# A diffusion step on one core: the value projections in 512 moving columns

## The reference

```
p = h @ w_in + b_in
(mq, mk, mv, mo, mi, mf, cb, cc, ch, nq, nk, nv, gt) = split(p)
y_ml = head_rms(mlstm_bidir(mq, mk, mv, ...)) * sigmoid(mo)
y_na = attention(nq, nk, nv, context cache, bias)
y_cv = cb * short_conv(cc * ch)
```

## Time and profile before

| | us |
|---|---|
| median of 3 runs | 3045.52 |
| lowest, highest | 3039.61, 3046.49 |
| the profiled execution | 3044.11 |
| its span | 3042.3 |
| TensorE busy | 2907.7 (96%) |
| VectorE, ACT, GpSimd busy | 1775.2 (58%), 1372.1 (45%), 544.8 (18%) |

### The profile page before, as it was taken

One profiled execution on the slowest core, in us unless ns is written; L12 is line 12 of the kernel. 1 busy time (PEld: TensorE's weight loads), 2 busy tenths in 40 slices (PEclk: granted clock), 3 DMA queues, 4 the chain that ended last, 5 costly groups with the idle time before them and its releaser, 6 DMA issues.

```text
span 3042.3 us, 41344 instructions
## 1 busy us (share of the span) xinstructions
PE 2907.7 (96%) x17186; PEld 2364.0 (78%) x17186; DVE 1775.2 (58%) x2039; ACT 1372.1 (45%) x1759; POOL 544.8 (18%) x215
## 2 busy tenths in 40 slices
PE   5999999999989999999989999999999899999998
PEld 4979888888976666767669798999998667676765
DVE  3550335134347889897966513351242798889897
ACT  2153321111137777776750533201101776777775
POOL 2504313232320000000024143242332100000000
PEclk9999999999999999999999899999999999999999
DMA  9423545475518989897975234423343597989896
GB/s 265 82 42 70 102 127 153 153 195 152 187 30 300 347 283 345 276 347 265 345 227 91 38 66 98 85 42 58 72 80 118 180 346 277 345 287 343 284 340 231
DMA packets 333691, 583.84 MB, mean 192 GB/s; under 512 B 14208, under 2 KB 98176, under 8 KB 333376
## 3 DMA queue, kind: packets, MB, share of 16 engines
q1 hardware_dynamic: 291312, 500.21, 54.6%
q10 hardware_dynamic: 33888, 60.04, 6.0%
q0 software_dynamic: 8304, 20.95, 2.1%
HBM read 567.49 MB, written 9.45 MB: 190 GB/s over the span
## 4 chain that ended last, share of the span: by engine, by line
PE 83%; DMA 5%; DVE 4%; ACT 3%; issue 2%; POOL 1%; SPq 1%; DVEq 1%; ACTq 0%; POOLq 0%
PE ps L861 26%; PE ps L1369 10%; PE ps L1372 10%; PE ps L1377 9%; PE ps L825 6%; PE ps L905 3%; PE ps L1138 2%; PE ps L1286 2%; DMA ring<-w_down 2%; DMA arena<-ada_w 2%; DMA ring<-w_gate 1%; PE ps L1119 1%; PE ps L929 1%; PE ps L1036 1%; PE ps L887 1%
## 5 line engine op out<-in xcount | busy, mean ns | idle before, releaser
L2344 DVE TENSOR_TENSOR w_lo<-ring,w_hi 128x2048 fp32r<-128x2048 f32 x256 | 583.9, 2287 | 97.4 <-ACT w_hi L1496 97.0
L1496 ACT ACTIVATE w_hi<-ring 128x2048 fp32r<-128x2048 f32 x256 | 487.0, 1910 | 81.3 <-DMA ring<-w_up 24.6
L861 PE MATMUL ps<-h_hi,w_hi 128*128 128x320 f32 x1632 | 511.2, 313 | 6.2 <-POOL w_lo L700 3.4
L861 PE MATMUL ps<-h_lo,w_hi 128*128 128x320 f32 x1632 | 507.7, 311 | 0.0
L861 PE MATMUL ps<-h_hi,w_lo 128*128 128x320 f32 x1632 | 507.7, 311 | 0.0
L698 POOL CAST w_hi<-ring 128x2048 fp32r<-128x2048 f32 (+1 forms) x74 | 141.3, 1910 | 1463.5 <-PE ps L1377 644.9
L700 POOL TENSOR_TENSOR w_lo<-ring,w_hi 128x2048 fp32r<-128x2048 f32 (+1 forms) x74 | 345.2, 4665 | 41.9 <-issue 36.2
L861 PEld LDWEIGHTS ps<-h_hi,w_hi 128*128 128x128 f32 x1632 | 309.7, 190 | 12.6 <-issue 9.9
L2344 DVE TENSOR_TENSOR w_third<-ring,w_third 128x2048 fp32r<-128x2048 f32 x128 | 293.1, 2290 | 40.8 <-ACT w_third L1496 40.0
L1559 ACT ACTIVATE arena<-ps,par 128x640 f32<-128x640 f32 x80 | 63.4, 795 | 561.7 <-PE ps L861 548.2
L861 PEld LDWEIGHTS ps<-h_lo,w_hi 128*128 128x128 f32 x1632 | 309.8, 190 | 0.0
(11 more groups left out here) (334 smaller groups left out, 5481.8 us busy)
## 6 DMA issues: line engine op xcount, KB each, us to landing
ring<-w_gate SPq DMA_DIRECT2D x128, 1024.0 KB, 6.2
ring<-w_up SPq DMA_DIRECT2D x128, 1024.0 KB, 6.0
ring<-w_down SPq DMA_DIRECT2D x128, 1024.0 KB, 6.9
ring<-w_in SPq DMA_DIRECT2D x64, 1024.0 KB, 13.1
arena<-ada_w ACTq DMA_DIRECT2D x40, 1024.0 KB, 7.0
arena<-ada_w SPq DMA_DIRECT2D x8, 1024.0 KB, 15.9
arena<-biasT ACTq DMA_DIRECT2D x16, 512.0 KB, 5.7
ring<-w_o SPq DMA_DIRECT2D x8, 1024.0 KB, 11.8
```

What stands on the lines that cost most here:

```text
L861: last = pe.matmul(ps[:, bank(u) + half, 0:HALF], w[:, k, f0:f0 + P], a[:, k, at], start=(k == 0 and part == 0), stop=(k == KD - 1 and par ...
L1496: act.activation(w_his[g % NW], ring[:, ff_slot(l, g), :], ACT.Copy).then_inc(ff_hi_ready.sem, 1)
L2344: dve.tensor_tensor(w_los[g % NW], ring[:, s, :], w_his[g % NW].bitcast(F32), ALU.subtract).then_inc(slot_used[s], 1)
```

## The change

`project_tokens` is turned inside out. A chunk of V's weights is now four k tiles of all 512 columns (rows 0 to 511 of `w_in`, then rows 512 to 1023) and a matmul has 512 columns. All five tiles take the first chunk, then all five the second, so five banks are open at once: tile 4 takes the odd bank beside tile 0's (`token_bank`). The first chunk is done with at tile 0 of the second round and the second at tile 4, and `ends` says so. On GpSimd the split of the first convolution chunk moves from behind the band loads to ahead of the stores of the attention's V.

```diff
+        def token_bank(u0, t):
+            return bank(u0 + t) if t < 4 else bank(u0) + 1
...
         for j in range(2):
-            ends[R_MV + j], ends[R_NV + j] = U_MV + NTILE - 1, U_NV + NTILE - 1
+            ends[R_MV + j], ends[R_NV + j] = U_MV + 4 * j, U_NV + 4 * j
...
-                        load(l, q + j, rows_of(win_l, c + CC * j))
+                        if q in (R_MV, R_NV):
+                            load(l, q + j, rows_of(w_in[l, 512 * j:512 * (j + 1), :], c, 512))
+                        else:
+                            load(l, q + j, rows_of(win_l, c + CC * j))
...
                 split(l, R_NV)
+                split(l, R_CONV, 1)
...
                 band_load(0)
                 band_load(1)
-                split(l, R_CONV)
+                split(l, R_CONV + 1, 1)
...
-                two = {}
-                for t, j in [(t, 0) for t in range(4)] + [(t, 1) for t in range(4)] + [(4, 0), (4, 1)]:
-                    if j == 0:
-                        free_unit(l, u0 + t)
-                    if j not in two:
-                        two[j] = split_chunk(l, q + j)
-                    _, hi, lo = two[j]
-                    at = slice(t * P, (t + 1) * P)
-                    for k in range(KD):
-                        for part, (a, w) in enumerate(((h_hi, hi), (h_lo, hi), (h_hi, lo))):
-                            last = pe.matmul(ps[:, bank(u0 + t), j * CC:(j + 1) * CC], a[:, k, at], w[:, k, :],
-                                             start=(k == 0 and part == 0), stop=(k == KD - 1 and part == 2))
-                    if j == 1:
-                        last.then_inc(unit_full.sem, 1)
+                for kh in range(2):
+                    for t in range(NTILE):
+                        if kh == 0 and t < 4:
+                            free_unit(l, u0 + t)
+                        if t == 0:
+                            hi, lo = (w.rearrange("p k n -> p (k n)").rearrange("p (k n) -> p k n", n=512)
+                                      for w in split_chunk(l, q + kh)[1:])
+                        at = slice(t * P, (t + 1) * P)
+                        for k in range(4):
+                            kk = 4 * kh + k
+                            for part, (a, w) in enumerate(((h_hi, hi), (h_lo, hi), (h_hi, lo))):
+                                last = pe.matmul(ps[:, token_bank(u0, t), :], a[:, kk, at], w[:, k, :],
+                                                 start=(kk == 0 and part == 0), stop=(kk == KD - 1 and part == 2))
+                        if kh == 1:
+                            last.then_inc(unit_full.sem, 1)
```

More of the change, by code:

```diff
@@ L2056, in norm_heads, with add_row_bias @@
                         .then_inc(head_normed.sem, 1)
-            def add_row_bias(l, u, out, at):
-                dve.wait_ge(*filled(l, u))
-                return dve.tensor_tensor(out, ps[:, bank(u), :], par[:, Q_BV + at:Q_BV + at + WB], ALU.add)
+            def add_row_bias(l, u0, t, out, at):
+                dve.wait_ge(*filled(l, u0 + t))
+                return dve.tensor_tensor(out, ps[:, token_bank(u0, t), :], par[:, Q_BV + at:Q_BV + at + WB], ALU.add)
             def attention(l):
@@ L2445, in _ @@
                     dve.tensor_tensor(mvx[:, t, :, 0:P],
-                                      ps[:, bank(U_MV + t), :].rearrange("p (h v) -> p h v", h=HM),
+                                      ps[:, token_bank(U_MV, t), :].rearrange("p (h v) -> p h v", h=HM),
                                       par[:, Q_BV:Q_BV + WB].rearrange("p (h v) -> p h v", h=HM), ALU.add)\
@@ L2462, in _ @@
                     out = nvp if t == 0 else nvst[:, t % 2, :]
-                    add_row_bias(l, U_NV + t, out, WB).then_inc(dve_emptied.sem, 1)
+                    add_row_bias(l, U_NV, t, out, WB).then_inc(dve_emptied.sem, 1)
                     dve.drain()
```

## The result

| | before | after |
|---|---|---|
| median, us | 3039.61 (5 runs) | 3055.05 (5 runs) |
| lowest, highest | 3033.63, 3046.49 | 3054.84, 3062.17 |
| the profiled execution, its span | 3044.11, 3042.3 | 3054.84, 3053.0 |

The change makes the kernel slower: the ratio is 1.0045, with a 95% interval of 1.0026 to 1.0064. The prediction's sum was 3054.9, its range 3041 to 3064.

What follows compares the result with a forecast made beforehand. TensorE, busy 96% of the span, was taken as the bound. From the profiled 3044.11 us: mLSTM blocks -2.4, attention starts +8.7 and +9.3, stall -2.4 twice, together +10.8, giving 3054.9; range 3041 to 3064.

Steps and rivals of the forecast that it cites:

- The matmuls: Value projections: 512-column matmuls at 230 ns, 1.2 us less a block; 2.4 us gained over the two mLSTM blocks.
- The Trainium skill's 131 ns: Sustained 512-column matmul pace: a block would take some 15.7 us, the sum 3031; the prediction judged the trace against it.
- The mLSTM's split: Split of the O gate's first chunk runs earlier, beside TensorE's V work; costed at nothing.
- The split ahead of the stores: Before attention: tile 1's store issued 4.4 us late and landing 4.9 us slower; starts lose 8.7 and 9.3 us.
- the landing: Tile 1's store, issue to landing: 6.4 and 7.55 us plus 4.9 for the ring load; upper end 9.7 more.
- Rivals 1 and 2: Ring load beside stores: first, stores untouched, 3045, 33%; second, bias loads held back and stores land faster, 3037, 7%.
- rival 1: Before attention: the ring load might be served first and does not touch the stores; sum 3045, chance 33%.
- The Trainium skill's turns between queues: DMA engines take equal turns among three queues: landing 9.6 us, 3.2 more instead of 4.9; sum 3051.5.
- The stall: First convolution piece no longer waits for w_lo; VectorE stays held, so 2.4 us gained in each layer.
- The distance that I took as fixed: From attention's start to the second chunk's subtraction: unchanged in the new order, so VectorE stays held and the gain is 2.4.
- The sum: mLSTM blocks -2.4, attention starts +8.7 and +9.3, stall -2.4 twice: +10.8 us, 3054.9; chance 54%.

Runs made afterwards that it cites:

- e1: The changed kernel with the first convolution split put back behind the band loads, 512 columns kept; ratio to the kernel before 1.0004.
- e2: The changed kernel with the ring load held until the stores of tiles 1 and 2 have landed; ratio to the kernel before 1.0054.
- e4: The changed kernel with ring load and bias loads both held until the stores of tiles 1 and 2 have landed; ratio to the kernel before 1.0019.
- e9: The kernel before (256 columns) with bias loads held and the cast's semaphore replacing the drain in the two convolution splits; ratio to the kernel before 0.9961.
- e3: The changed kernel with only the bias loads held until the stores of tiles 1 and 2 have landed; ratio to the kernel before 1.0038.
- e8: The changed kernel with split back behind band loads, bias loads held, cast's semaphore replacing the drain in both convolution splits; ratio to before 0.9937, median 3022.94 us.
- e11: e8 run once more, on the same chip as e9; ratio to the kernel before 0.9919, median 3019.53 us.

## Why the prediction held, and where it did not

The cause is the one predicted, and the sum came out within a us of the median; its terms did not all hold. The mechanism is shown by e1 (the split's move is the whole loss) and by e2 and e4 (the store's landing sets the start of attention).

**1. The matmuls.** 226.8 ns, the upper of the two gains considered (the extrapolated 227, not the measured 230 of the experts): 1.6 us a block instead of 1.2. It counts in the mLSTM and not in the attention's block, as said; e9 shows that it counts there once the store is out of the way. The Trainium skill's 131 ns ("TensorE: Matmul & The Clock Gate", "Back-to-back issue gap") is not met in this kernel.

**2. The mLSTM's split.** Nothing in layer 0: from 115.35 to the next block at 308.88 the kernel after took 193.5 us, before from 115.12 to 310.23 195.1, and the 1.6 between them is the block. In layer 1 the difference is 2.4 us; the 0.8 beyond the block goes with TensorE's granted clock, 0.75 over 13 us of the mLSTM's stage before (1687 to 1700) and 0.84 after (1688 to 1701).

**3. The split ahead of the stores.** VectorE's L2064 was held 3.92 us and ended 0.7 us behind the subtraction (predicted 0.55); the store went out at +26.1 from the block's start (predicted +25.7). The term that was mis-sized is the landing: 16.1 us in both layers, against 11.3 and 12.5. I had added the ring load's own DMA time, 4.9; the row of a bias load that had met ring loads said 9.7, and it was right (16.1 - 6.4 = 9.7 in layer 0, 16.1 - 7.55 = 8.6 in layer 1). My reason for not taking it, that there two loads had been freed ahead and here one, was wrong: e3 and e4 show that one is enough, and in that row, too, only one went ahead. The two ring loads of the kernel before were issued at 359.33 and 365.90, the bias load at 359.4. The first of them landed after 15.9 us, where the one with nothing beside it took 8.1; the price of such a meeting stood in the trace. SP's timeline, and landings of ring loads issued from 340 to 362 and from 305 to 330:

```profile
359.33 6.93 SPq L643 DMA_DIRECT2D ring<-w_in  x2
```

```profile
ring<-w_in SPq DMA_DIRECT2D x1, 1024.0 KB, 15.9
...
ring<-w_in SPq DMA_DIRECT2D x1, 1024.0 KB, 8.1
```

So what failed is the step that priced the meeting at the 4.9 us of DMA time that a ring load needs alone. The same 1040 packets now took 48.6% of 27 us (325 to 352), 13.1 us of all 16 engines, and the stores came behind them:

```profile
q1 hardware_dynamic: 1040, 1.05, 48.6%
```

Attention started at +44.0 where the prediction's sum has +38.7 and +39.8, so the starts cost 14.0 and 13.5 us, not 8.7 and 9.3. Rivals 1 and 2 fall with it: the ring load was served first, as rival 1 has it, but at a pace that made the stores wait. The Trainium skill's turns between queues ("DMA: Bandwidth & Descriptors", "Queues, rings and completion order"), read as equal time, gave 3.2 us more instead of 9.7. It speaks of turns by packet; the trace shows no turn of the stores in the 11 us from 334 to 345.

**4. The stall.** Gone in both layers. In layer 1 VectorE's L2086 was held (4.32 us) and the gain was 22.5 - 20.2 = 2.3 us, as worked out. In layer 0 it was not held (0.17): GpSimd waited 3.50 us for the last store instead of 2.41, its pause was 7.22 us instead of 6.49, and so its second subtraction began at 369.22, after L2086. The gain was 22.4 - 17.5 = 4.9 us, 1.3 of it because the twelve matmuls of the convolution piece ran at the upper clock (1.86 us instead of 3.15). The distance that I took as fixed, 14.6 us from attention's start to that subtraction, was 16.4.

**5. The sum.** By these terms the loss up to the last weighing is 133.1 - 124.0 = 9.1 us in layer 0 and 137.5 - 124.9 = 12.6 in layer 1, less 1.6 each for the mLSTM: 18.5 us, and not 10.8. Layer 1 has 1.4 us in it that no term named (12.6 against 13.5 - 2.3): the rest of its attention began at a lower granted clock, 0.80 in this window where the kernel before had 1.00:

```profile
1904.00:1912.00 8.00, 7.17 (x48) 6.77 (x48) 3.25 (x11) 2.55 (x7) 0.00 (x0) 0.80 0.98 144
```

The two profiled runs differ by 10.7 all the same, for a reason that is not in the prediction. From the last weighing of layer 0 to layer 1's second value projection the kernel before took 1404.0 us and the one after 1395.8, 8.2 less, of which the mLSTM explains 2.4 (part 2); 1.4 more are won behind layer 1's last weighing. Over all thirteen traces that stretch scatters from 1395.8 to 1407.4 (e1 1398.9, e8 1399.1, and e11, the same code as e8, 1396.4); the chain of waits leads there through loads of expert weights again and again. So I take the rest for scatter; no run tests it. Over many runs the ratio of 1.0045 means 13.7 us (7.9 to 19.5), which holds the 18.5 and the 10.8. That the number fits to 0.2 us is partly luck: the two starts were priced 9.5 us too low, the two traces differ by 7.2 us the other way in stretches that the change does not touch (8.2 - 2.4, and 1.4), and the forecast started from a profiled run of 3044.11 us, 4.5 above the median of the five runs (3039.61), so that the medians differ by 15.4 us. The sign and the cause are not luck.

## What to carry to other kernels

Who moves a step that frees a buffer moves the transfer which that buffer was holding back: list what is in flight at the new place, and price the meeting by a row in which such transfers did meet (here the 15.9 us of a ring load before the change), not by the load's DMA time alone. Before a step is moved to get out of a stall, look at what the stall is made of; here it was a drain behind the engine's own DMAs, and a wait on the one instruction that mattered was worth more than any place for the split. An edit that wins nothing in the whole (e1) can win once its cover is gone (e9 against e8), so test the parts of a change apart.

## What the runs showed of the hardware

- The ring load of 1 MB in pieces of 1 KB, issued shortly ahead of other transfers, kept the DMA engines at a share of 1.0 while they moved 63 to 89 GB/s, 0.21 us a packet against 0.08 alone; in after from 334 to 345 nothing else moved. A store of 256 KB landed in 14.9 to 16.1 us beside it, in 6.4 beside two bias loads, in 3.2 beside other stores alone. With the ring load in pieces of 2 KB it was 10.3.
- GpSimd's drain behind its own band loads lasted from 6.5 us (before) to 9.4 us (e4); a wait on the cast's semaphore in the same place 0.1 us. What the drain waits for beyond the cast was not tried.
- After the block TensorE's granted clock fell from 1.00 through 0.63 to 0.50, the lower of its two levels (1.2 GHz), within the 16.44 us in which it stood still; the first eight matmuls of attention then took 1.23 us instead of 0.72.
